# Modulation columns of a transformer front, formed by TensorE in four column groups instead of by VectorE

## The reference, cut to what matters

```python
c_act = jax.nn.silu(c)
mod = c_act @ w_mod[l] + b_mod[l]                 # [2048] @ [2048, 6144]
shift, scale, gate = jnp.split(mod, 3, axis=-1)
h = rmsnorm(x, norm_gain[l]) * (1.0 + scale[:, None, :]) + shift[:, None, :]
proj = h @ w_in[l]
...
bias = rel_bias[t5_bucket(pb[:, :, None] - ps)]   # 32 buckets, 8 heads
```

## Time and profile before

| | us |
|---|---|
| median of 3 runs | 1870.92 |
| the runs | 1869.0 to 1870.99 |
| the profiled execution, its time | 1869.93 |
| its span | 1868.1 |
| TensorE busy in the span | 1826.4 |
| VectorE busy | 1351.8 |
| ScalarE busy | 990.8 |
| POOL busy | 203.0 |

### The profile page before, as it was taken

One profiled execution on the slowest core, in us unless ns is written; L12 is line 12 of the kernel. 1 busy time (PEld: TensorE's weight loads), 2 busy tenths in 40 slices (PEclk: granted clock), 3 DMA queues, 4 the chain that ended last, 5 costly groups with the idle time before them and its releaser, 6 DMA issues.

```text
span 1868.1 us, 25006 instructions
## 1 busy us (share of the span) xinstructions
PE 1826.4 (98%) x9520; PEld 1512.4 (81%) x9520; DVE 1351.8 (72%) x1949; ACT 990.8 (53%) x1359; POOL 203.0 (11%) x256
## 2 busy tenths in 40 slices
PE   5989999999999999999999999999999999999997
PEld 3768788889888878888888888888888888888886
DVE  6979999988987778857765544488885466665555
ACT  6664455446447445544654644476765445444464
POOL 0000002100000000210000000044441020031001
PEclk9989999999999999999999999999999999999999
DMA  9989978965986986744365555554555555557562
GB/s 350 373 323 343 332 232 302 322 224 182 330 297 229 361 280 225 235 159 159 124 225 185 182 199 192 191 181 161 177 178 182 185 191 184 184 180 248 182 197 94
DMA packets 211826, 424.07 MB, mean 227 GB/s; under 512 B 7680, under 2 KB 12684, under 8 KB 210316
## 3 DMA queue, kind: packets, MB, share of 16 engines
q1 hardware_dynamic: 209788, 414.94, 65.6%
q10 hardware_dynamic: 1936, 7.76, 1.0%
HBM read 418.45 MB, written 4.21 MB: 226 GB/s over the span
## 4 chain that ended last, share of the span: by engine, by line
PE 91%; DMA 3%; DVE 2%; ACT 2%; issue 1%; SPq 0%; DVEq 0%; POOLq 0%; POOL 0%; ACTq 0%
PE acc L684 28%; PE acc L686 28%; PE acc L685 28%; DMA raw<-in_w_in 2%; DVE scr L2078 1%; DMA raw<-in_w_mod 1%; PE tps L725 1%; PE tps L765 1%; ACT w_hi L1418 0%; ACT proj L1393 0%; PE sps L996 0%; PE tps L988 0%; PE sps L952 0%; PE sps L893 0%; PE sps L892 0%
## 5 line engine op out<-in xcount | busy, mean ns | idle before, releaser
L1859 DVE TENSOR_TENSOR w_lo<-raw,w_hi 128x1024 fp32r<-128x1024 f32 (+1 forms) x580 | 721.1, 1249 | 444.8 <-ACT w_hi L1246 442.5
L1246 ACT ACTIVATE w_hi<-raw 128x1024 fp32r<-128x1024 f32 (+1 forms) x580 | 606.1, 1050 | 762.3 <-PE acc L686 684.3
L684 PE MATMUL acc<-w_hi,ht_hi 128*128 128x512 f32 (+1 forms) x2304 | 910.5, 395 | 0.5 <-issue 0.4
L686 PE MATMUL acc<-w_hi,ht_lo 128*128 128x512 f32 (+1 forms) x2304 | 894.2, 388 | 0.0
L685 PE MATMUL acc<-w_lo,ht_hi 128*128 128x512 f32 (+1 forms) x2304 | 892.3, 387 | 0.0
L686 PEld LDWEIGHTS acc<-w_hi,ht_lo 128*128 128x128 f32 x2304 | 432.4, 188 | 90.3
L684 PEld LDWEIGHTS acc<-w_hi,ht_hi 128*128 128x128 f32 x2304 | 432.9, 188 | 87.4 <-issue 3.2
L685 PEld LDWEIGHTS acc<-w_lo,ht_hi 128*128 128x128 f32 x2304 | 433.3, 188 | 83.4
L1989 DVE SCALAR_TENSOR_TENSOR scr<-raw,vcol,scr 128x512 f32<-128x512 f32 x154 | 110.9, 761 | 4.8 <-issue 0.4
L2078 DVE SCALAR_TENSOR_TENSOR scr<-raw,vcol,scr 128x1024 f32<-128x1024 f32 x56 | 68.0, 1278 | 6.6 <-DMA raw<-in_w_mod 6.6
L1989 DVE SCALAR_TENSOR_TENSOR proj<-raw,vcol,proj 128x512 f32<-128x512 f32 x70 | 52.3, 788 | 1.9
(11 more groups left out here) (305 smaller groups left out, 1446.8 us busy)
## 6 DMA issues: line engine op xcount, KB each, us to landing
raw<-in_w_in SPq DMA_DIRECT2D x208, 1024.0 KB, 5.1
raw<-in_w_mod SPq DMA_DIRECT2D x64, 1024.0 KB, 6.2
raw<-in_w_mod SPq DMA_DIRECT2D x64, 512.0 KB, 6.3
raw<-in_w_out SPq DMA_DIRECT2D x32, 1024.0 KB, 5.2
raw<-in_w_o SPq DMA_DIRECT2D x16, 1024.0 KB, 5.2
raw<-in_w_ple_gate SPq DMA_DIRECT2D x16, 1024.0 KB, 5.1
raw<-in_w_b_out SPq DMA_DIRECT2D x8, 1024.0 KB, 5.1
raw<-in_w_a_out SPq DMA_DIRECT2D x8, 1024.0 KB, 5.1
```

What stands on the lines that cost most here:

```text
L684: pe.matmul(o, hi_m, w_hi[:, slot, u, 0:width], start=start, stop=False)
L686: mm = pe.matmul(o, lo_m, w_hi[:, slot, u, 0:width], start=False, stop=stop)
L1246: act.activation(w_hi[:, x % SPL, :, 0:width], raw[:, j, 2 * (x % halves):2 * (x % halves) + 2, 0:width], ACT.Copy).then_inc(hi_ready, 1)
L1859: dve.tensor_tensor(w_lo[:, x % SPL, :, 0:width], raw[:, j, 2 * (x % halves):2 * (x % halves) + 2, 0:width], w_hi[:, x % SPL, :, 0:width]. ...
```

## The change

The modulation sums move from VectorE to TensorE. The operand that stays in the array is one column of `c`, repeated 32 times, and the weights of a slot stream by as they landed, in fp32. The four products of a slot (two groups of 128 rows, shift and scale) go to four column groups of 32 and write four groups of partitions of one bank, `tps[:, 1, :]`, in which the eight slots of a quarter are summed. VectorE copies that bank to `mrows` (`rows_out`), and `pair_sums` turns it into columns with four products by a selector `picks` of two columns. A slot is free when TensorE has read it (`mod_read`), and SyncE waits by number (`slot_free`).

TensorE reads the first two slots of quarter `i + 1` ahead of the burst of quarter `i`, two after each of its first two half quarters and one after each of the others.

ScalarE forms two tiles right behind each of the first two high parts, so ahead of the steps `a` and `b`; VectorE's `columns` and `tiles_low` move with them.

The lookup becomes bf16: the one-hot matrix is bf16, and the table is split by POOL, in five small linked operations, in three bf16 parts that add up to it; each lookup product becomes three.

```diff
+        rb_parts = proj[:, 0, 5312:5312 + 3 * KPG * NH // 2].bitcast(BF16).rearrange("p (b n) -> p b n", b=3)
...
+            def slot_free(t):
+
+                i, j = divmod(t - RAW, 10)
+                if t < RAW:
+                    return
+                if j < 8:
+                    sp.wait_ge(mod_read, 8 * i + j + 1)
+                else:
+                    sp.wait_ge(raw_read, 8 + 4 * i + 2 * (j - 7))
...
-                        mm = pe.matmul(bias_cols[:, c:c + KPG * NH], onehot[:, n % 2, e * w + m * P:e * w + (m + 1) * P],
-                                       rb_diag, start=True, stop=True)
+                        for b in range(3):
+                            mm = pe.matmul(bias_cols[:, c:c + KPG * NH], onehot[:, n % 2, e * w + m * P:e * w + (m + 1) * P],
+                                           rb_parts[:, b, :], start=b == 0, stop=b == 2)
...
+            def mod_slot(i, j):
+
+                t = 10 * i + j
+                if j == 0:
+                    pe.wait_ge(mod_taken, 1 + 2 * i)
+                pe.wait_ge(raw_landed[t % RAW], landed_start(t))
+                for u in range(2):
+                    c_col = v2("c", 2 * j + u).broadcast_to([P, 32])
+                    for b in range(2):
+                        g = 32 * (2 * b + u)
+                        mm = pe.matmul(tps[g:g + 32, 1, :], c_col, raw[:, t % RAW, 2 * u + b, :], start=j == 0, stop=j == 7)
+                mm.then_inc(mod_read, 1)
...
-                for b in range(2):
-                    for j in range(4):
-                        mm = pe.matmul(tps[:, 1, 4 * b + j:4 * b + j + 1], macc[:, b, 0, j * P:(j + 1) * P], ones,
-                                       start=True, stop=True)
+                for j in range(4):
+                    mm = pe.matmul(tps[:, 1, 2 * j:2 * j + 2], mrows[:, j * P:(j + 1) * P], picks, start=True, stop=True)
...
-            steps(0, 3)
+            mod_slots(0, 0, 2)
+            steps(0, 1)
+            mod_slots(0, 2, 1)
+            steps(1, 1)
+            mod_slots(0, 3, 1)
             pe.wait_ge(s_vec, 16 * 10)
...
-            steps(3, n - 3)
+            steps(2, n - 2)
+            mod_slots(0, 4, 2)
             pe.wait_ge(vec_ready, 2)
             turn_rows(0)
+            mod_slots(0, 6, 1)
             turn_rows(2)
+            mod_slots(0, 7, 1)
             pe.wait_ge(acc_taken, taken.next(2))
             for i, (a, b, inside) in enumerate(STEPS):
                 pair_sums()
                 steps(n, a + b)
                 n += a + b
-                lo.skip(16)
+                mod_slots(i + 1, 0, 2)
                 for q, (g, h) in enumerate(((0, 0), (0, 1), (1, 0), (1, 1))):
                     quarter_half(i, g, h)
                     steps(n, inside[q])
                     n += inside[q]
                     if i < 3 and q < 2:
                         turn_rows(4 * (i + 1) + 2 * q)
+                    mod_slots(i + 1, 2 + 2 * q if q < 2 else 4 + q, 2 if q < 2 else 1)
...
                         act.activation(w_hi[:, 2 * g + h, :, :], raw[:, t % RAW, 2 * h:2 * h + 2, :], ACT.Copy)\
                            .then_inc(hi_ready, 1)
+                        if g == 0:
+                            formed_tiles(4 * i + 2 * h)
                 steps(n + a, b)
                 n += a + b
-                formed_tiles(i)
...
+            def rows_out(i):
+
+                dve.wait_ge(mod_summed, m_free.next(2))
+                dve.wait_ge(mod_read, 8 * (i + 1))
+                dve.tensor_copy(mrows, tps[:, 1, :]).then_inc(mod_ready, 1)
...
+            buckets()
+            row_sum()
+            row_inverse()
+            bound_ratio()
             for i in range(4):
...
+                rows_out(i)
+                columns(i)
                 for g in range(2):
```

More of the change, by code:

```diff
@@ L69 @@
 C_PW = C_HPI + 1
-C_TH = C_PW + 2
+C_SEL = C_PW + 2
+C_TH = C_SEL + 2
 C_N = C_TH + NB - EXACT - 1
@@ L528, in _ @@
             free = Seen(sp, raw_read)
+            def slot_free(t):
[6 more added lines that the diff above has]
+                    sp.wait_ge(raw_read, 8 + 4 * i + 2 * (j - 7))
             def mod_pair(i, j):
                 slot = (10 * i + j) % RAW
-                sp.wait_ge(raw_read, free.next(2))
+                slot_free(10 * i + j)
                 for b in range(2):
@@ L570, in _ @@
                 for g in range(2):
-                    land((10 * i + 8 + g) % RAW, full(wi[0])(i, CHUNKS[g] * CH, CH))
+                    slot_free(10 * i + 8 + g)
+                    slot = (10 * i + 8 + g) % RAW
+                    sp.dma_start(raw[:, slot, :, :], full(wi[0])(i, CHUNKS[g] * CH, CH)).then_inc(raw_landed[slot], 16)
+            free.skip(16)
             for l in range(DEPTH):
@@ L799, in _ @@
             pe.wait_ge(buckets_ready, 1)
[L800 removed]
+            pe.wait_ge(rb_split, 1)
             spread_keys(0)
+            pe.wait_ge(vec_ready, 1)
             def steps(n, count):
@@ L1385, in scaled_rows, with formed_tiles @@
                                    scale=st[:, 22 + m:23 + m]).then_inc(xs_ready, 1)
[L1387 to L1396, removed]
+            def formed_tiles(k):
+                act.wait_ge(columns_ready, k // 4 + 1)
+                for e in range(2):
+                    scale, bias_col = of_layer(0)(k + e)
+                    act.activation(xt(k + e), xt(k + e), ACT.Identity, scale=scale, bias=bias_col).then_inc(tiles_formed, 1)
+                act.wait_ge(tiles_formed, k + 2)
+                act.activation(ht_hi[:, k:k + 2, :], xt(k, 2).rearrange("p (e t) -> p e t", e=2), ACT.Copy)\
+                   .then_inc(turn_hi, 2)
             n = FIRST_STEPS
@@ L2087, in tiles_low @@
                                   ht_hi[:, k:k + 2, :].bitcast(F32), ALU.subtract).then_inc(turn_lo, 2)
-            dve.wait_ge(mod_summed, m_free.next(2))
-            for u in range(2):
-                modulate(0, 0, u)
-            for i in range(4):
-                for j in range(1, 8):
-                    for u in range(2):
-                        modulate(i, j, u)
-                    if i == 0 and j == 1:
-                        buckets()
-                    if i == 0 and j == 2:
-                        row_sum()
-                    if i == 0 and j == 3:
-                        row_inverse()
-                    if i == 0 and j == 6:
-                        bound_ratio()
-                dve.wait_ge(raw_read, own.ahead(0))
-                dve.tensor_tensor(macc[:, :, 0, :], macc[:, :, 0, :], macc[:, :, 1, :], ALU.add).then_inc(mod_ready, 1)
+            for t in range(40):
+                m_land[t % RAW].skip(32 if t % 10 < 8 else 16)
+            buckets()
+            row_sum()
+            row_inverse()
+            bound_ratio()
+            for i in range(4):
+                rows_out(i)
+                columns(i)
                 for g in range(2):
                     t = (10 * i + 8 + g) % RAW
-                    m_land[t].skip(16)
                     for h in range(2):
-                        if g and h:
-                            columns(i)
                         dve.wait_ge(hi_ready, hi.next())
@@ L2115, in _ @@
                         own.skip(1)
-                for e in range(2):
-                    if i < 3:
-                        if e == 0:
-                            dve.wait_ge(mod_summed, m_free.next(2))
-                        modulate(i + 1, 0, e)
-                    tiles_low(4 * i + 2 * e)
+                        if g == 0:
+                            tiles_low(4 * i + 2 * h)
             results.skip(16)
```

40 lines of the change are left out of this document (23 added, 17 removed).

## The result

| | before | after |
|---|---|---|
| median, us | 1870.95 (4 runs) | 1896.42 (4 runs) |
| the profiled execution, its time | 1869.93 | 1897.57 |
| its span | 1868.1 | 1895.7 |

The runs of after lie from 1895.15 to 1898.87. The recorded estimate of the ratio is 1.0143 (95% interval 1.013 to 1.0155), the quotient of the two medians 1.0136: by the medians the kernel became 25.5 us slower; the forecast was 1904.8 with a range from 1887 to 1925.

A forecast was written before the change was run, and what follows sets the result against it. TensorE's unbroken run bounds the kernel, its start paced by transfers before: 40.5 + 15.1 + 3 x 24.4 + 2 x 15.8 + 4.9 = 165.3 against 130.4, +34.9 on 1869.9, giving 1904.8 us; range 1887 to 1925.

The forecast's parts named there:

- second and third burst: First product to the next quarter's last modulation slot: 24.4 us each, 0.4 of it added for the low clock.
- The opening: Start of kernel to the first quarter's last modulation slot: 40.5 us, between 44.4 all low clock and 38.
- The slot: TensorE's four fp32 products per modulation slot, column groups side by side: 0.87 us, 1.07 alone, 1.94 for two.
- Rival (3): Column groups on TensorE overlap only in part: a slot of 1.13 us, +8, 1913 us; chance 0.15.
- Rival (2): Column groups on TensorE take turns: a slot of 3.5 us instead of 0.87, +84, 1989 us; chance 0.04.
- The lookup: Twelve bf16 products on TensorE: at most 0.68 us, 0.2 if 32 columns alone counted; a step taken at 0.9.
- The pause: Last modulation slot to next burst: 15.8 us from columns 2.5, ScalarE 8.9, lookup 0.9, two slots 3.5.
- rival (4): Clock stays high through pauses (3 x 1.75), opening (2.5) and bursts (1.2): -9, 1896 us; chance 0.17.
- The last pause: Fourth quarter, without steps or slots: 4.9 us from columns 2.5, two tiles 1.70, low part 0.69.
- DMA adds nothing: Front transfers: slots freed late by TensorE still land ahead of it; the tightest, free at 12.3, is wanted at 21.
- comes from order, not from work: In the pause, the main cost is ScalarE's program order: 8.9 us before the one-hot matrix is there.
- Signs: Expected profile: DMA share near 0.7, TensorE idle some 9 us a quarter, VectorE under half busy, 1737 us after the start.

The follow-up runs named there:

- e4: Changed kernel with 28 of the 32 modulation slots read by one column group alone; 1964.95 us, ratio 1.0506.
- e2: Changed kernel with STEPS alone changed: no step ahead of a burst, those steps put inside it; 1901.63 us, ratio 1.0167.
- e1: Changed kernel with ScalarE's tiles formed after both steps again and VectorE's low parts of the tiles after those of w_in; 1883.51 us, ratio 1.0078.

## Why the prediction was right, and where its sizes were off

The predicted start of the unbroken run was 165.3; it was 156.87. Term by term, from the windows of after:

| term | predicted | measured | off |
|---|---|---|---|
| opening, to the last slot of the first quarter | 40.5 | 36.6 | -3.9 |
| first pause | 15.1 | 14.8 | -0.3 |
| first burst | 24.4 | 25.2 | +0.8 |
| second and third pause | 31.6 | 30.1 | -1.5 |
| second and third burst | 48.8 | 44.3 | -4.5 |
| last pause | 4.9 | 5.9 | +1.0 |
| sum | 165.3 | 156.9 | -8.4 |

Behind the start came 1.1 us more, so the profiled execution shows +27.6 where +34.9 was forecast, and the medians +25.5. The mechanism held in the pauses, which carry most of the loss. The hit doesn't rest on errors that cancel: the misses are 10.2 us one way and 1.8 the other.

**The opening** is the largest miss of a single stretch. I took a value between low clock throughout and a high clock from 31 on. The first two slots did run at the low clock's pace (3.64 us, as at 47.86, where 0.50 is granted), though the profile's rows give 1.00 for 18.60 to 22.20. But the slot at 23.75 already took 1.06 us, the high clock's time, at a granted 1.00 up to 36.6. So TensorE kept up, and the last slot stands at 35.56 behind a DMA wait of 0.90: at its end the opening goes at the pace of the transfers, and 36.6 is below the least that I allowed (38). The same caution holds for the first half quarter of before, which I called one at the low clock: its 5.27 us are that clock's pace, while the earlier trace rows show 1.00.

**The slot** was sized right: 0.87 us of products for one, 1.94 for two was 1.86. The four groups run side by side. The records of two slots say it plainly: four start within 0.02 us (56.212 to 56.232), the next fours at 56.665, 57.094 and 57.523, so four records of 512 columns take the 0.43 us that the earlier trace rows give for two of 256, one behind the other. The two changes of form, for which 0.2 were taken, are in the 0.14 that 1.86 is over four times 0.43; the earlier trace rows as shown don't hold the product ahead of the change, so they bounded it less well than I wrote. Rival (3), a partial overlap, is out: it wanted 1.13 a slot. The figure beside it in the Trainium skill, "TensorE: Matmul & The Clock Gate", Measured speedup vs the span model, is 2.38 times for three column groups, and my estimate from it was a fifth lost. This trace doesn't bear that out: four groups came to 3.7 times one (1.92 us against 7.05 in e4). Rival (2) was priced at 3.5 us a slot, and e4 built it: 7.05 for two.

**The lookup** was sized too high. Twelve bf16 products were bounded by 0.68 from rows of 128 columns and taken near that; from their start to the next operation are 0.31 us (55.34 to 55.65), about 26 ns each, nearer the 0.2 that I named as the other end and did not take. A single step between half quarters is 0.54 instead of 0.9. Three single steps a burst make 1.0 of the 2.2 us by which the second and third burst were forecast too long, and the block of two steps makes 0.8 (2.32 for 3.1, from 106.03 to 108.35; 2.87 in the first burst). The rest is the added 0.4 for a first half quarter at the low clock, which these bursts did not have, and 0.3 in the slots; against it, the two turns of rows took 0.3 more (0.56 each for 0.39). The first burst had the low clock twice (at 51.43 and from 70.82, granted 0.50) and so came out over.

**The pause** is the part that held best. Columns 2.5 us after the slot (76.60 to 79.11), as forecast; ScalarE 9.0 (79.15 to 88.17) for 8.9; then the lookup 0.5 for 0.9 and two slots 2.9 for 3.5, in all 14.95 for 15.8. The waits named it nearly as the prediction did: what waits 24.1 us for ScalarE's step is the spread of keys right ahead of the lookup, and what releases it is the first of the two one-hot operations. The clock fell to 0.60 and 0.66, so rival (4), though its number, 1896, is the nearest of all to what was measured, is right only in part. Its largest term, 5.25 us in the pauses, came to 1.2 (two slots 2.9 for 3.5 in two of them). Its 2.5 in the opening and part of its 1.2 in the bursts did come: the clock was high from 23.75 on, and at the start of the second and third burst. The rest of the 8.4 us came from a cheap lookup. So its number is near for a mixture of reasons, some its own.

**The last pause** has 1.0 more: ScalarE waited 0.37 between forming and the high part, and the columns came 2.9 after the slot instead of 2.5; the rest are handoffs.

**"DMA adds nothing"** held for this kernel (0.9 us of TensorE's waits), but only because its pauses are long; e2 shows 16.1 us of waits as soon as they shrink. In the first pause the transfers are a bound right behind ScalarE, at a DMA share of 1.00: there the order put back brought 2.2 us and not 7. My statement that the main cost "comes from order, not from work" was too strong. With the order put back 13 us remain: a quarter of e1 takes 31.5 us, a burst of 23.9 with six slots in it and a pause of 7.6 with two slots at the low clock in it (3.57 us). TensorE is busy for 28.6 of the first quarter's 31.5 and 26.8 of the second's 31.3, so its own work alone comes near or over the 27.5 of the transfers, and its waits of 2.9 and 4.6 stand on top. VectorE's sums of before ran beside the burst; on TensorE they stand in line with it.

**Signs.** DMA share between 50 and 160 us near 0.7: it was 0.79, with 0.97 in the second and third burst and 0.55 and 0.60 in the pauses between them. TensorE idle 9 us a quarter, mostly before the spread ahead of a lookup: 8.75 in the pause from 76.60 (14.95 less 6.20 busy). VectorE below half busy: 19.4 of 110 us. The run behind it the same within 1.1.

What stays open is how much of e1's 13 us falls on the low clock and how much on the slots themselves; no run held the clock high through a pause.

## What to carry to other kernels

Work that is taken from an engine beside the bottleneck and given to the bottleneck is paid for, even if it is cheap there (0.9 us for a slot instead of 2.5), unless it moves what sets the pace; here a quarter took 28.0 us where the transfers alone need 27.5, so freeing VectorE could give little.

When an engine's program is reordered, look for work without a dependence that is put behind work with one: here two steps of the lookup, which need no columns, behind tiles that wait for them, cost 13 to 16 us by themselves. The order brought something only where no step stands between, in the fourth quarter (1.8 us of pause).

Ring buffers held by a slow consumer are a second queue: shortening the pause by 7 us, with no step left ahead of the burst, brought 16 us of waits for slots (6.7 of them in the first pause, where the transfers are a bound anyway).

## What the runs showed of the hardware

- Four fp32 products with 32 columns of the array each and 512 streamed columns run side by side: 0.43 us for four records; two slots, sixteen records, take 1.92 us, in one group 7.05.
- Twelve bf16 products of 32 columns with 128 rows start within 0.31 us, about 26 ns apart; the eight fp32 records that they replace take 0.81 in the kernel before., with 57 ns for 128 columns, had led me to twice as much.
- TensorE's granted clock was 0.60 to 0.66 in pauses in which it was busy for 6 of 15 us, and at 1.00 in the second and third burst from their first products on, after two modulation slots; in the pause ahead of the first burst the same two slots did not raise it (3.57 us at a granted 0.50, which lasted into the burst's first products, 0.42 apart).
